# A mixture-of-experts layer on one core: eight experts with fixed tiles instead of four, and their token table made ahead of the order of the rest

## What is computed

```python
def hier_moe(h, ...):                      # 544 rows of 1024
    lg = hf @ w_rg + b_rg                  # 4 groups, the best one is taken
    le = hf @ w_re + b_re                  # 8 experts in each group
    top_p, top_i = top_k(softmax(le_sel), 2)
    for e in range(32):
        he = silu(hf @ w_gate[e]) * (hf @ w_up[e])      # 1024 -> 256
        out = out + combine[:, e:e + 1] * (he @ w_down[e])
```

## Time and profile before

| | before |
|---|---|
| device time, median of 3 runs | 967.47 us (964.45 to 967.98) |
| profiled execution, first to last instruction (span) | 963.2 us |
| median less span | 4.3 us |
| busy: PE, DVE, ACT, POOL | 845.6, 509.0, 190.9, 168.8 us |
| moved by DMA | 204.16 MB, mean 212 GB/s |

### The profile page before, as it was taken

One profiled execution on the slowest core, in us unless ns is written; L12 is line 12 of the kernel. 1 busy time (PEld: TensorE's weight loads), 2 busy tenths in 40 slices (PEclk: granted clock), 3 DMA queues, 4 the chain that ended last, 5 costly groups with the idle time before them and its releaser, 6 DMA issues. The chain is left out here.

```text
span 963.2 us, 12133 instructions
## 1 busy us (share of the span) xinstructions
PE 845.6 (88%) x4994; PEld 618.5 (64%) x4994; DVE 509.0 (53%) x753; ACT 190.9 (20%) x284; POOL 168.8 (18%) x156
## 2 busy tenths in 40 slices
PE   2899999999998879979999999917999987979776
PEld 1688886347997879978878644605666655545432
DVE  1328999999999443351365543481333331222236
ACT  3211211111233121741120011201111110101003
POOL 1000000000045454143223000001122221121110
PEclk9899999999998889989999999856999998989899
DMA  9923225011332131365999593242999999999936
GB/s 323 315 64 88 65 67 174 1 44 44 89 88 57 48 88 45 88 219 175 316 314 322 186 381 149 97 193 83 411 404 416 415 418 394 368 406 394 373 110 248
DMA packets 112600, 204.16 MB, mean 212 GB/s; under 512 B 9484, under 2 KB 68212, under 8 KB 104350
## 3 DMA queue, kind: packets, MB, share of 16 engines
q1 hardware_dynamic: 94192, 159.36, 46.5%
q10 hardware_dynamic: 12830, 34.93, 9.6%
q0 software_dynamic: 5520, 9.06, 2.5%
HBM read 199.49 MB, written 14.84 MB: 223 GB/s over the span
## 5 line engine op out<-in xcount | busy, mean ns | idle before, releaser
L858 PE MATMUL PS<-arena 128*64 128x256 f32 (+1 forms) x1056 | 148.7, 411 | 30.2 <-issue 25.7
L1280 DVE SCALAR_TENSOR_TENSOR arena<-arena,VT 128x574 f32<-128x574 f32 x240 | 175.1, 811 | 0.0
L858 PEld LDWEIGHTS PS<-arena 128*64 128x64 f32 (+1 forms) x1056 | 108.8, 156 | 65.4 <-issue 36.9
L1695 POOL TENSOR_TENSOR wL<-arena,wH 128x1024 fp32r<-128x1024 f32 x32 | 83.2, 2621 | 360.8 <-ACT wH L998 360.8
L552 PE MATMUL PS<-arena 128*128 128x272 f32 x512 | 119.1, 396 | 1.6 <-DVE arena L1242 1.6
L552 PEld LDWEIGHTS PS<-arena 128*128 128x128 f32 x512 | 98.3, 192 | 22.1 <-issue 1.6
L619 PE MATMUL PS<-gH,wH 128*128 128x272 f32 x384 | 83.0, 299 | 9.1 <-POOL wL L1695 5.5
L1591 DVE TENSOR_TENSOR arena<-PS,arena 128x256 f32<-128x256 f32 x19 | 8.1, 424 | 140.1 <-ACT arena L1114 140.1
L619 PE MATMUL PS<-gL,wH 128*128 128x272 f32 x384 | 81.9, 296 | 0.0
L619 PE MATMUL PS<-gH,wL 128*128 128x272 f32 x384 | 81.7, 294 | 0.0
L878 PE MATMUL PS<-arena 128*64 128x512 f32 (+1 forms) x264 | 69.1, 597 | 1.4 <-DVE arena L1595 1.4
(11 more groups left out here) (282 smaller groups left out, 996.9 us busy)
## 6 DMA issues: line engine op xcount, KB each, us to landing
arena<-w_gate SPq DMA_DIRECT2D x32, 1024.0 KB, 7.3
arena<-w_up SPq DMA_DIRECT2D x32, 1024.0 KB, 15.4
arena<-w_down ACTq DMA_DIRECT2D x28, 1024.0 KB, 13.9
arena<-w_in SPq DMA_DIRECT2D x40, 512.0 KB, 5.2
arena<-w_ada SPq DMA_DIRECT2D x8, 2048.0 KB, 14.4
vecs<-w_ada SPq DMA_DIRECT2D x4, 2048.0 KB, 9.3
arena<-x_prompt SPq DMA_DIRECT2D x8, 512.0 KB, 8.0
arena<-w_in SPq DMA_DIRECT2D x4, 1024.0 KB, 6.3
```

The costliest lines, as they stand in the source:

```text
L858: last = pe.matmul(PS[h * rows:(h + 1) * rows, 2, n * DE:(n + 1) * DE], hG[:, b, k * SLOTS + h * rows:k * SLOTS + (h + 1) * rows], buf[r / ...
L1280: dve.scalar_tensor_tensor(out=total, in0=src, scalar=tap, in1=total, op0=ALU.mult, op1=ALU.add).then_inc(conv_step, 1)
L1695: pool.tensor_tensor(wL2[q % 2][:, m], WP[q % 2][:, m], wH2[q % 2][:, m], ALU.subtract).then_inc(gw_split, 1)
```

## The change

- `NSTATIC` is 8: experts 0 to 7 have tiles 1 to 4, two in each. The alternation of single and paired tiles begins at tile 5. There are 19 tiles and 32 loads as before.
- Their tokens come from a table of their own (`Rs`, `static_ready`, `static_ps`), made as soon as the ranks are known; `tokI` of tiles 1 to 4 is written from it (`static_known`), and POOL waits for that alone.
- PE starts tile 1 without waiting for `routed`, and makes the other tables (`dynamic_tables`) between gate_up(1) and turn_rows(2). The three tables of token, pair and weight are one product with 84 columns in place of one with 28 and one with 56.
- On SP, loads 4 and 5 (experts 4 and 5) go out after gate_up(1) with no wait for routing and no look into `owner`; `routed` and the two `g2b` loads come ahead of load 6, `owned` ahead of load 8.
- ACT takes both halves of the turned rows of tiles 1 and 2. Its waits for `routed`, `owned` and `g2_in` come after take_rows(2) and ahead of scale_g2(1).
- DVE no longer takes rows of tiles 1 and 2. It makes the hidden product of tile 1 ahead of its wait for the tables.
- `sil`, `he`, `heT`, `g2b` and `gfb` change their places in SBUF, since the routing tables are still in use during tile 1.

```diff
-NSTATIC, NWIDE = 4, 5
+NSTATIC, NWIDE = 8, 5
...
-        sil = view(O_T + 2048, DE)
-        he = view(O_T + 2048 + DE, DE)
+        sil = view(O_T + 6096, DE)
+        he = view(O_T + 6096 + DE, DE)
...
-            sp.wait_ge(routed, 1)
             for p in range(2):
                 sp.wait_ge(mod_stored[p], 16 * 6)
-            for s in range(2):
-                sp.dma_start(g2b[s], mod_vec(5, P, s)).then_inc(g2_in, 16)
-            sp.wait_ge(owned, 1)
             for n in range(4, LOADS):
+                if n == 6:
+                    sp.wait_ge(routed, 1)
+                    for s in range(2):
+                        sp.dma_start(g2b[s], mod_vec(5, P, s)).then_inc(g2_in, 16)
+                if n == NSTATIC:
+                    sp.wait_ge(owned, 1)
                 sp.wait_ge(gu_done, last_use[n - 4])
-                load_owned(unit_of(n), n % 4)
+                if n < NSTATIC:
+                    load_gu(n % 4, slice(n, n + 1))
+                else:
+                    load_owned(unit_of(n), n % 4)
...
-            pe.wait_ge(tab_ready, 1)
-            table_of(2, 0, TILES)
-            pe.wait_ge(own_tab, 1)
-            pe.matmul(PS[0:1, 3, 0:P], own_col[:, 0:1], ident[:, :], start=True, stop=True).then_inc(own_ps, 1)
-            pe.wait_ge(tab_ready, 2)
-            table_of(6, TILES, 3 * TILES)
+            pe.wait_ge(static_ready, 1)
+            table_of(5, Rs, NSTATIC // 2).then_inc(static_ps, 1)
+
+            def dynamic_tables():
+                pe.wait_ge(own_tab, 1)
+                pe.matmul(PS[0:1, 4, 0:P], own_col[:, 0:1], ident[:, :], start=True, stop=True).then_inc(own_ps, 1)
+                pe.wait_ge(tab_ready, 1)
+                table_of(6, R, 3 * TILES).then_inc(tab_ps, 1)
...
                 gate_up(None, first, slot(first))
+                if first == 1:
+                    dynamic_tables()
                 turn_rows(None, first + 1, slot(first + 1))
...
-            pe.wait_ge(routed, 1)
             expert_tiles(1, ALWAYS)
...
                 act.activation(hG[:, b, 0:512], PS[:, 0, :], ACT.Copy).then_inc(hg_ready, 1)
+                if i is None and t <= 2:
+                    act.activation(hG[:, b, 512:1024], PS[:, 1, :], ACT.Copy).then_inc(hg_ready, 1)
...
                 take_rows(None, first + 1, slot(first + 1))
+                if first == 1:
+                    act.wait_ge(routed, 1)
+                    act.wait_ge(owned, 1)
+                    act.wait_ge(g2_in, 32)
                 scale_g2(None, first, slot(first))
...
+            then(dve.tensor_reduce(flat["rank"], prod, AX, ALU.add))
+            soon(dve.tensor_tensor(FOH, wide(flat["rank"].unsqueeze(2), P, 2 * TT, CAP), wide(iota[:, 0:CAP].unsqueeze(1), P, 2 * TT, CAP), ALU.is_equal))
+            for h in range(2):
+                ins = dve.tensor_tensor(Rs[:, :, h * NSTATIC // 2:(h + 1) * NSTATIC // 2], pair_oh[:, :, h:NSTATIC:2],
+                                        wide(vals[:, 0].rearrange("p k t -> p (k t)").unsqueeze(2), P, 2 * TT, NSTATIC // 2), ALU.mult)
...
+            dve.sem_inc(static_ready)
...
             then(dve.tensor_reduce(j, higher, AX, ALU.add))
+            dve.wait_ge(static_ps, 1)
+            then(dve.tensor_scalar(un[:, 0:NSTATIC // 2], PS[0:SLOTS, 5, 0:NSTATIC // 2], 0.0, 4096.0, ALU.is_equal, ALU.mult))
+            dve.scalar_tensor_tensor(out=tokI[:, 0:NSTATIC // 2], in0=PS[0:SLOTS, 5, 0:NSTATIC // 2], scalar=-1.0, in1=un[:, 0:NSTATIC // 2],
+                                     op0=ALU.add, op1=ALU.add).then_inc(static_known, 1)
...
             soon(dve.tensor_copy(owner[0:1, UNITS:UNITS + 1], upto[0:1, NE - 1:NE]))
+            gate_hidden(None, 1)
             dve.wait_ge(tab_ps, 1)
...
-                take_rows(None, first, slot(first))
-                gate_hidden(None, first)
-                take_rows(None, first + 1, slot(first + 1))
+                if first > 1:
+                    take_rows(None, first, slot(first))
+                    gate_hidden(None, first)
+                    take_rows(None, first + 1, slot(first + 1))
                 take_hidden(None, first)
...
-            pool.wait_ge(tokens_known, 1)
+            pool.wait_ge(static_known, 1)
             pool.wait_ge(h2_stored[0], 48)
```

More of the change, by code:

```diff
@@ L153, in build @@
         Y = view(O_T, 2, D)
[L154 to L156 removed]
+        sil = view(O_T + 6096, DE)
+        he = view(O_T + 6096 + DE, DE)
+        heT = view(O_T + 6096 + 2 * DE, 2, SLOTS)
         pair_rows = [view(O_A + 5120 * k, TT, D) for k in range(2)]
[L158 to L159 removed]
+        g2b = [view(O_T + 2048, D), view(O_T + 3072, D)]
+        gfb = view(O_T + 4096, D)
         at_w = [O_T]
@@ L264, in build @@
         routed = sem("routed")
-        tokens_known = sem("tokens_known")
+        static_ready, static_ps, static_known, tokens_known = sem("static_ready"), sem("static_ps"), sem("static_known"), sem("tokens_known")
         own_tab, own_ps, owned = sem("own_tab"), sem("own_ps"), sem("owned")
@@ L310, in build @@
         R = table(2 * TT, 2 * 3 * TILES)
+        Rs = table(2 * TT, NSTATIC)
         un = table(TILES)
@@ L356, in build @@
             first = in_tile[-1][-1] + 1 if t > 1 else 0
-            alone = 2 < t <= 2 + 2 * NWIDE and t % 2 == 1
-            again = t == 4
+            alone = NSTATIC // 2 < t <= NSTATIC // 2 + 2 * NWIDE and (t - NSTATIC // 2) % 2 == 1
+            again = t == NSTATIC // 2 + 2
             in_tile.append([first] if alone else [first - again, first + 1 - again])
@@ L812, in _, with table_of @@
             last.then_inc(rank_ps, 1)
-            def table_of(bank, first, last_col):
+            def table_of(bank, rows, per):
                 for n in range(2 * TT):
                     for h in range(2):
-                        last = pe.matmul(PS[h * CAP:(h + 1) * CAP, bank, 0:last_col - first], FOH[:, n, :],
-                                         R[:, n, h * 3 * TILES + first:h * 3 * TILES + last_col], start=(n == 0), stop=(n == 2 * TT - 1))
-                last.then_inc(tab_ps, 1)
-            pe.wait_ge(tab_ready, 1)
-            table_of(2, 0, TILES)
-            pe.wait_ge(own_tab, 1)
-            pe.matmul(PS[0:1, 3, 0:P], own_col[:, 0:1], ident[:, :], start=True, stop=True).then_inc(own_ps, 1)
-            pe.wait_ge(tab_ready, 2)
-            table_of(6, TILES, 3 * TILES)
+                        last = pe.matmul(PS[h * CAP:(h + 1) * CAP, bank, 0:per], FOH[:, n, :],
+                                         rows[:, n, h * per:(h + 1) * per], start=(n == 0), stop=(n == 2 * TT - 1))
+                return last
+            pe.wait_ge(static_ready, 1)
[5 more added lines that the diff above has]
+                table_of(6, R, 3 * TILES).then_inc(tab_ps, 1)
             def turn_rows(i, t, b):
@@ L1138, in expert_tile @@
                     for n in range(4, LOADS):
-                        if last_use[n - 4] == t - 1:
+                        if last_use[n - 4] == t - 1 and n < NSTATIC:
+                            act.dma_start(WD[n % 4 // 2][n % 2], w_down[n:n + 1].rearrange("o p k n -> (o p) k n")).then_inc(wd_full[n % 4], 16)
+                        elif last_use[n - 4] == t - 1:
                             load_d(unit_of(n), n % 4)
@@ L1503, in _ @@
                                           op0=ALU.mult, op1=ALU.add))
-            soon(dve.tensor_reduce(cum[:, 0, NE:2 * NE], cmp, AX, ALU.add))
-            then(dve.tensor_reduce(flat["rank"], prod, AX, ALU.add))
+            then(dve.tensor_reduce(cum[:, 0, NE:2 * NE], cmp, AX, ALU.add))
             then(dve.tensor_tensor(higher, wide(key[:, 0:1, :], P, NDYN, NDYN), wide(key[:, 0, :].unsqueeze(2), P, NDYN, NDYN), ALU.is_gt))
@@ L1515, in _ @@
             then(dve.scalar_tensor_tensor(out=j, in0=right, scalar=-float(NPAIR), in1=rnk, op0=ALU.mult, op1=ALU.add))
-            then(dve.tensor_scalar(low, j, 4.0, -float(4 * NWIDE - 6), ALU.mult, ALU.add))
+            then(dve.tensor_scalar(low, j, 4.0, float(NSTATIC - 4 * NWIDE + 2), ALU.mult, ALU.add))
             soon(dve.tensor_tensor(cum[:, 0, NE:2 * NE], cum[:, 0, NE:2 * NE], base[:, 1, :], ALU.subtract))
-            then(dve.tensor_scalar(both, j, 2.0, 4.0, ALU.mult, ALU.add))
+            then(dve.tensor_scalar(both, j, 2.0, float(NSTATIC), ALU.mult, ALU.add))
             soon(dve.tensor_scalar(cum[:, 0, NE:2 * NE], cum[:, 0, NE:2 * NE], 0.0, None, ALU.max))
@@ L1566, in _ @@
             soon(dve.tensor_copy(owner[0:1, UNITS:UNITS + 1], upto[0:1, NE - 1:NE]))
+            gate_hidden(None, 1)
             dve.wait_ge(tab_ps, 1)
-            then(dve.tensor_scalar(un[0:SLOTS, :], PS[0:SLOTS, 2, 0:TILES], 0.0, 4096.0, ALU.is_equal, ALU.mult))
-            dve.scalar_tensor_tensor(out=tokI[:, :], in0=PS[0:SLOTS, 2, 0:TILES], scalar=-1.0, in1=un[0:SLOTS, :],
+            toks, prs, wts = (PS[0:SLOTS, 6, n * TILES:(n + 1) * TILES] for n in range(3))
+            then(dve.tensor_scalar(un[0:SLOTS, :], toks, 0.0, 4096.0, ALU.is_equal, ALU.mult))
```

(10 more changed lines are left out.)

21 lines of the change are left out of this document (13 added, 8 removed).

## The result

The changed kernel took 954.2 us (median of 4 runs, 953.57 to 957.8), beside 967.73 for the kernel before (4 runs). The ratio is 0.9872, with a 95% interval of 0.9849 to 0.9895: by this ratio 12.4 us less, with 10.2 to 14.6 as the interval (the two medians lie 13.5 apart). Measured twice more with six runs each, on two different chips, it gave 0.9894 (0.9863 to 0.9924) and 0.9887 (0.9859 to 0.9915); the mean of the three ratios, 0.9884, is 11.2 us less. The forecast was 955.6, faster. The profiled execution of the changed kernel took 957.8 us with a span of 956.0.

The account below looks back on a forecast made before the run. Expert-weight transfers set the end, which moves with the stream's start. Starting 14.45 us earlier, less 2.6 for `g2b` in the stream, gave 11.9 us: 967.5 - 11.9 = 955.6 us, range 950.5 to 962.5.

Parts of the forecast that it names:

- The bound: Expert-weight transfers set the end, which moves with the stream's start, plus or minus what is added or leaves it idle.
- Rival A: TensorE's chain sets the end, gate_up(3) being only 9.6 us earlier: 957.9 us; chance 0.17.
- The cover: After 790 us, TensorE's 25.7 us of waiting for weights hide gate_up(3)'s smaller gain; without it, the end is 2.3 later.
- Fewer waits for weights at the end: Listed sign of being wrong; TensorE was expected to idle more than 20 us in the last tiles.
- Table of the fixed tiles: Ranks to `static_known`: `Rs` products 0.3 us, table product 2.35, tokens written at 638.9.
- First rows: From `tokI` to turn_rows(1): 4.8 us plus 0.4 for POOL being held by VectorE, so turning starts at 644.1.
- Start of gate_up(1): After turning and ACT's two copies, tile 1 starts at 647.45, 14.45 us earlier, and takes 9.44.
- Load 4: Loads 4 and 5 go out after gate_up(1), at 657.95, 14.45 us earlier.
- g2b in the stream: Its 1.05 MB behind loads 4 and 5 cost 2.6 us at 400 GB/s, landing at about 672.
- Rival D: `g2b` lands late, holding ACT ahead of scale_g2(1); gate_up(3) no earlier from a landing at 681.6; 972 us; chance 0.07.
- Dynamic tables: Behind gate_up(1), TensorE makes the tables in 2.0 us; `R` is ready 5.9 us before it is needed.
- Rivals B and C: B: low clock throughout gate_up(1), 959.3 us, chance 0.07. C: tile 1 hardly earlier or stream dry, about 967, chance 0.09.

Follow-up runs that it names:

- u7: u3 with the gate halves of loads 6 and 7 also released by the gate matmuls of gate_up(2); 948.49 us, ratio 0.9821 to the kernel before.
- u3: The changed kernel with the edits of u1 and u2 together; 952.7 us, ratio 0.9862 to the kernel before.
- b1: The kernel before with only the eight fixed experts, tables and waits as before; 969.33 us, ratio 1.0030.
- b2: The kernel before with only ACT's three waits (`routed`, `owned`, `g2b`) moved to ahead of scale_g2(1); 964.47 us, ratio 0.9976.
- u6: The changed kernel with SP's wait for routing and the `g2b` loads ahead of load 4 instead of load 6; 958.74 us, ratio 0.9923.
- u1: The changed kernel with the two `g2b` loads moved from ahead of load 6 to right after the logits; 952.0 us, ratio 0.9849 to the kernel before.
- u8: u7 with turn_rows(2) ahead of the dynamic tables on TensorE; 949.44 us, ratio 0.9816 to the kernel before.
- u2: The changed kernel with the gate halves of loads 4 and 5 released by the gate matmuls of gate_up(1); 954.32 us, ratio 0.9872 to the kernel before.
- u5: The changed kernel with `routed` and the `g2b` loads moved behind loads 6 and 7; 964.84 us, ratio 0.9994 to the kernel before.
- a1: The changed kernel measured again, unaltered, as the yardstick of the third set; 954.88 us, ratio 0.9887 to the kernel before.

## Why the prediction was right

- *The bound.* That the end goes with the stream's start, as long as it does not run dry, is shown by u7 against u3 and by the marks of all kernels. In the seven profiles with `g2b` ahead of load 4 or ahead of routing (before, b1, b2, u6, u1, u7, u8; u3 with its hole is left out), load 4 moves from +39.5 to +19.5, and from it to the end it is always 290.6 to 292.9 us; from gate_up(3) to the end it is 271.3 to 279.2. With `g2b` behind load 4 (the changed kernel three times, u2) it is 294.5 to 296.4. Rival A (TensorE's chain, 957.9) is out: the chain was 8.9 us ahead at gate_up(3) and 3.6 at gate_up(11), and the end still moved by 10.8 in that profile.
- *The cover.* TensorE's waits ahead of gate_up in the last tiles fell from 25.7 us to 20.2: by 5.5, where the two gains of the prediction leave 2.3. "Fewer waits for weights at the end" was one of its signs of being wrong. About as much lead, 5.3 us, was lost between gate_up(3) and gate_up(6), which the prediction had no term for; what was left of the cover was still enough.
- *Table of the fixed tiles.* `Rs` 0.31 (I took 0.3), product 2.30 (2.35), `tokI` was complete at 642.52, +6.0; the sum had 638.9, which is +6.0 too.
- *First rows.* From `tokI` to turn_rows(1) 4.85 us, 4.80 before. The 0.4 that I added for POOL being held was not there: its copies took 0.21 and 0.19, its issues 1.12 and 1.02. That does not speak against the hold in the earlier trace rows: the VectorE operations beside these steps took only 0.17 to 0.49 us. By the Trainium skill (SBUF — State Buffer, section "SBUF: two separate sides"), a VectorE operation with two SBUF inputs and a GpSimd operation that reads SBUF exclude each other for the whole instruction; here that could cost no more than such a length, and no row shows even that.
- *Start of gate_up(1).* 14.9 us earlier for 14.45 predicted. It took 8.92; in other profiles of the same stage it took from 8.78 to 10.08. The prediction had this spread only in its range.
- *Load 4.* 16.4 earlier for 14.45. Beside the two terms above, 1.0 us comes from a thing that I left out: before, 1.05 us lay between the end of gate_up(1) (671.35) and the issue, after it 0.09 (659.50 to 659.59). For loads 4 and 5 the expert's number is no longer read from `owner` by SP. Within the changed kernel it is the same: load 6, without that look, goes out 0.04 us after its matmuls, load 8, with it, 1.07. The text spoke of "no look into `owner`" but had no term for it.
- *g2b in the stream.* I took 2.6, and u1's profile gives 3.3. It landed 12 to 13.5 us after its issue and ACT went on after 14.0, where I had 11.7; so the stall ahead of gate_up(3) was 2.3 longer and cost the clock too. Little of it reached the end: u1, which takes out `g2b` and the stall together, ended 2.3 us sooner in the profile and 3.7 in the median, and 2.6 of that is for the bytes. Rival D, a late `g2b`, is real at about 1 us per us. In u5 `g2b` let ACT go on at +49.3 and gate_up(3) was at +52.8, 0.4 later than before. So the turning point lies near +48.9, in the time of the profile before at 681.8; the prediction put it at 681.6.
- *Dynamic tables.* 0.38 and 1.67, together 2.0 as taken; the cover for `R` was 4.9 us (654.64 to 659.5).
- *Rivals B and C* did not occur. B's half did in a way: the clock is what spreads gate_up(1) between 8.8 and 10.1 (the mean granted clock over it was 0.81 where it took 8.78, in u5, and 0.70 where it took 10.02, in a1).
- *One step was poorly put*: that the median lies 4.3 us above the span. Span and device time of one execution differ by 1.8 us (957.8 and 956.0), so the profiled execution before took about 965.0, 2.5 less than the median. Made against that, the sum gives 965.0 - 11.9 = 953.1, and the shift of 3.6 us of the front part makes 956.7 of it, where 957.8 was measured.

- *Slips in the working.* The low end of the range adds up to 950.7 (955.6 - 2.3 - 2.6), not 950.5. "Half of the matmuls ran full" in rival B should be 43 of 63 records. And `g2b` was taken to go out at 660.3, which is 0.3 ahead of `routed`, for which it waits. None of these changes the forecast.

The size, 11.9 us, is close to what was measured (12.4, 10.3 and 10.9 by the three ratios, 11.5 by the profiles). That is in part luck, for it came from terms that were each off by 0.5 to 2 us and balanced: 1.5 more at the start of the stream, and 1.9 more in the stretch and the tail. For the 1.2 us of the stretch beyond `g2b` the windows give a hint: at the same 399 GB/s, 239.1 us before are 95.4 MB and 243.5 after are 97.2, so 1.8 MB more passed between the two marks, where `g2b` is 1.05. Which transfers the rest are was not looked at, and single profiles of one kernel differ by as much (242.1 to 243.5). So they do in the tail, whose 0.7 us stay unexplained (51.8 to 52.9).

## What to carry to other kernels

Where a long stream of transfers sets the end, ask first when it starts and whether it ever runs dry: here an earlier start paid one for one until the queue was empty, and then only releasing the buffers in smaller parts helped. A transfer that many others wait for, here 1 MB of `g2b`, is best put in a gap before the stream if there is one that does not delay its start: inside the stream it costs its own time, and here it arrived 12 to 13.5 us after its issue, behind the 4 MB that were queued ahead of it. And if profiles are to be compared within a few us, count from a mark right ahead of the changed part.

## What the hardware showed beyond what was expected

- The untouched front part of 633 us varies by 7.6 us between executions (632.0 to 639.6 us to the ranks' product, over 14 profiles). In the three profiles of the changed kernel it spreads by 6.9 us and the whole span by 6.3, so there it is the run-to-run spread; what causes it was not found.
- Reading an expert's number from SBUF on SP ahead of a transfer puts about 1 us on the path (1.05 against 0.09 us from the matmuls' end to the issue; the read itself shows as 0.28 to 0.48 us).
- A stall of TensorE of 3.9 us ahead of gate_up(3) cost 2.4 us more in the 64 matmuls behind it (9.54 for 7.13), the granted clock being 0.50 (1.2 GHz) for the first 4 us of them. Since TensorE waits for weights later on, little or nothing of this is seen at the end.
